# One transformer-block kernel: the rings of split weights begin 64 bytes later than the activations, modulo 128

## What is computed

```
mod = silu(c) @ W_ada + b                      # six vectors of 2048
h   = rmsnorm(x) * (1 + scale1) + shift1
P   = h @ W_in                                 # 2048 x 4944
      -> 8 attention heads (low-rank q and kv, softmax over 512 keys)
      -> 4 mLSTM heads, forward and backward, chunk 128
x   = x + gate1 * (concat(heads) @ W_out)      # 2048 x 2048
h2  = rmsnorm(x) * (1 + scale2) + shift2
x   = x + gate2 * (relu(h2 @ W1)^2 @ W2)       # 2048 x 8192, 8192 x 2048
```

## Time and profile before

| | us |
|---|---|
| median of 2 runs | 2275.3 (2273.9 and 2276.7) |
| span of the profiled execution | 2274.7 |
| TensorE busy (PE) in it | 2224.7 |
| weight loads (PEld) in it | 1859.0 |
| GpSimd busy | 1224.3 |
| VectorE busy | 1508.9 |
| ScalarE busy | 859.9 |

### The profile page before, as it was taken

The page is one execution under the profiler, slowest core; times in us unless marked ns, Lnnn a source line. Parts: engine busy times, 40 slices in busy tenths (PEclk is TensorE's granted clock), DMA queues, the critical chain, the costliest instruction groups (busy, mean ns, idle before and its releaser), DMA issues.

```text
span 2274.7 us, 26399 instructions
## 1 busy us (share of the span) xinstructions
PE 2224.7 (98%) x10292; PEld 1859.0 (82%) x10292; DVE 1508.9 (66%) x1506; ACT 859.9 (38%) x1152; POOL 1224.3 (54%) x521
## 2 busy tenths in 40 slices
PE   6999999999998999999999999999999999999999
PEld 6888888888887878888888888888888888888887
DVE  5876976775646687446687677678666556656756
ACT  5435454533356222333333333333333333333331
POOL 2004344342521455267776766777776667676763
PEclk9999999999999999999999999999999999999999
DMA  9966355454636687444443444343433333333342
GB/s 348 319 219 227 127 184 192 146 201 164 240 130 238 245 286 269 141 127 134 130 126 128 128 128 132 121 149 111 130 111 102 108 96 102 112 94 107 101 170 102
DMA packets 185465, 365.52 MB, mean 161 GB/s; under 512 B 15354, under 2 KB 40444, under 8 KB 183296
## 3 DMA queue, kind: packets, MB, share of 16 engines
q1 hardware_dynamic: 176992, 340.79, 45.5%
q10 hardware_dynamic: 8352, 23.07, 2.7%
HBM read 332.33 MB, written 31.48 MB: 160 GB/s over the span
## 4 chain that ended last, share of the span: by engine, by line
PE 87%; DVE 6%; issue 2%; DMA 2%; ACT 1%; POOL 1%; SPq 1%; DVEq 0%; ACTq 0%; POOLq 0%
PE ps L852 19%; PE ps L853 19%; PE ps L854 19%; PE ps L1345 8%; PE ps L1344 8%; PE ps L1346 8%; DVE acc L1967 1%; DMA araw<-in_w_ada 1%; PE ps L886 1%; PE ps L913 1%; PE ps L1142 1%; DVE acc L2018 1%; DVE rt L2278 1%; DVE qn L2270 0%; SPq L459 0%
## 5 line engine op out<-in xcount | busy, mean ns | idle before, releaser
L396 POOL TENSOR_TENSOR wlo<-wraw,whi 128x1024 fp32r<-128x1024 f32 (+3 forms) x112 | 280.8, 2519 | 465.4 <-ACT whi L391 438.3
L844 POOL TENSOR_TENSOR wlo<-wq,whi 128x1024 fp32r<-128x1024 f32 x150 | 387.0, 2582 | 123.6 <-ACT whi L1859 123.6
L844 POOL TENSOR_TENSOR wlo<-wraw,whi 128x1024 fp32r<-128x1024 f32 x132 | 381.2, 2888 | 33.8 <-ACT whi L1859 33.8
L852 PE MATMUL ps<-h2T,whi 128*128 128x512 f32 x1024 | 398.6, 389 | 0.0
L854 PE MATMUL ps<-h2T,wlo 128*128 128x512 f32 x1024 | 398.4, 389 | 0.0
L853 PE MATMUL ps<-h2T,whi 128*128 128x512 f32 x1024 | 398.3, 389 | 0.0
L2612 DVE TENSOR_TENSOR yacc<-ps,yacc 128x1024 f32<-128x1024 f32 x202 | 246.4, 1220 | 215.9 <-PE ps L1346 213.2
L1344 PE MATMUL ps<-whi,ahi 128*128 128x512 f32 x840 | 326.9, 389 | 0.2 <-DVE yacc L2612 0.2
L1346 PE MATMUL ps<-whi,alo 128*128 128x512 f32 x840 | 326.8, 389 | 0.0
L1345 PE MATMUL ps<-wlo,ahi 128*128 128x512 f32 x840 | 326.8, 389 | 0.0
L1859 ACT ACTIVATE whi<-wq 128x1024 fp32r<-128x1024 f32 x150 | 159.1, 1060 | 354.1 <-PE ps L854 223.3
(11 more groups left out here) (340 smaller groups left out, 3995.4 us busy)
## 6 DMA issues: line engine op xcount, KB each, us to landing
araw<-in_w_ada SPq DMA_DIRECT2D x144, 512.0 KB, 5.8
wraw<-in_w_ff SPq DMA_DIRECT2D x136, 512.0 KB, 3.8
wq<-in_w_ff SPq DMA_DIRECT2D x120, 512.0 KB, 4.2
wraw<-in_w_in SPq DMA_DIRECT2D x72, 512.0 KB, 5.8
arawx<-in_w_ada SPq DMA_DIRECT2D x48, 512.0 KB, 4.7
wraw<-in_w_out SPq DMA_DIRECT2D x32, 512.0 KB, 7.0
xnat<-in_x ACTq DMA_DIRECT2D x4, 1024.0 KB, 8.5
xT_d<-xT ACTq DMA_DIRECT2D x1, 4096.0 KB, 13.3
```

The lines of the kernel that those rows point to most:

```text
L396: pool.tensor_tensor(wlo[:, slot, 0:kb, 0:cols], wraw[:, slot, 0:kb, 0:cols], whi[:, slot, 0:kb, 0:cols].bitcast(F), ALU.subtract).then_in ...
L844: pool.tensor_tensor(wlo[:, slot, :, :], raw, whi[:, slot, :, :].bitcast(F), ALU.subtract).then_inc(lo_ready, 1)
L852: pe.matmul(dst, lhs[0], rhs[0], start=start, stop=False)
```

## The change

Two allocations grow. A filler `pad_w` of 64 bytes stands ahead of `wraw`, and each `under_...` tile grows by 64 bytes:

```
+    at(perm, "pad_w", [P, 16])
     wraw = at(perm, "wraw", [P, RING, KB, 512])
     whi = at(perm, "whi", [P, RING, KB, 512], R)
...
             if kb:
-                at(st, f"under_{tiles[0][0]}", [P, int(kb * 256)])
+                at(st, f"under_{tiles[0][0]}", [P, int(kb * 256) + 16])
             return [at(st, *tile) for tile in tiles]
```

## The result

The changed kernel takes 2318.8 us (median of 2 runs, 2315.6 and 2322.1) against 2275.3: 1.88% slower, ratio 1.0188 with a 95% interval of 1.0171 to 1.0204. It lies 44 us over the forecast and 0.8 us over the top of my range. The profiled execution took 2322.1 us, of which 2320.3 are its span, 45.6 us more than the span of before.

What follows compares the result with a forecast made beforehand. The prediction took TensorE's matmul count times pace as the bound. Its sum, 0 on the matmuls and 0 +/- 3 us on the start, left the 2274.7 us span unchanged: forecast 2275 us, range 2266 to 2318.

Steps and rivals of the forecast that it cites:

- Bound: Whole kernel: TensorE's matmuls fill 98% of the span, so time is the number of matmuls times their pace.
- The pace and its bounds: Ring-tile matmuls: a fixed 13.3 ns beside the columns; 8,781 matmuls, effect bounded from -117 to +117 us.
- The term that the sum put at 0: The change's effect on the pace of the ring-tile matmuls, taken as 0 us.
- Why zero between those bounds: Ring-tile matmuls: two arguments that a start 64 bytes different leaves the pace unchanged, 0 us.
- The first: Load and stream in ring matmuls: their distance drifts some 530 bytes per load, passing every distance modulo 128 about four times.
- The second leg: Transposes from `ckv`, half its rows off by 64: 110 ns each against 109 from aligned `cq`, so no slower load.
- 0.80: Chance given to no change for the whole kernel, at 2268 to 2283 us.
- The rule of two independent ports: TensorE has two independent read ports and never waits on anyone, so the shift is worth 0 us.
- The 96 us: Possible gain on 8,781 matmuls if 10.9 ns each above the formula's 215.8 were contention cured by the shift.
- What else moves: ScalarE, GpSimd, VectorE and clock unaffected; DMA in the start phase 0 with a margin of 3 us.
- The slower one: Shift brings collisions to ring matmuls: persisting 231 ns pace, 40 us, 2315 us, chance 0.06; doubled fixed part 2392 us.
- The faster rival: Fixed part of ring matmuls shrinks: 2158 us if all 13.3 ns go, 2217 if half; chance 0.08.

Runs made afterwards that it cites:

- the probe: Layer left out, series of 64 matmuls alone at varied distances and column counts; with 448 columns 202.5 ns at distance 0, 202.2 at 64.
- e1: Against the kernel before, ring tiles and activation tiles all moved by 64 bytes, distance still 0; 2274.5 us.
- e6: Against the kernel before, rings in place, activation tiles moved by 256 bytes; 2275.7 us.
- e2: Against the kernel before, rings in place, activation tiles moved by 64 bytes; 2316.5 us.
- e3: Against the kernel before, rings in place, activation tiles moved by 128 bytes; 2322.0 us.
- e7: Against the kernel before, only the high ring tile `whi` (with the small tables behind it) moved by 64 bytes; 2320.2 us.
- The bf16 series: Two series of 64 matmuls alone in bf16, layer left out, at distances 0 and 64; 215.9 ns a matmul at 64, starts 215 to 216 apart at 0.

## Why the prediction was wrong

**Bound.** Right. The time is the number of matmuls times their pace, and 39 of the 45.6 us are that pace.

**The pace and its bounds.** Right as far as the rows went: 13.3 ns beside the columns at 336, 384 and 512, none at half clock, and bounds from -117 to +117 us, inside which the +45.6 us lies. As a rule for any number of columns it is not right: the probe has 15.9 ns at 448. The term that the sum put at 0 measured 4.7 ns a matmul, 39 us.

**Why zero between those bounds.** This is the step that failed, in both its legs. The first said that two streams which drift through every distance in one load can't care where they start. The runs show that they do: e1 and e6 against e2, e3 and the change. The argument looks at one matmul and its load by themselves. The runs show that one feeds into the next. At a distance of 0 the starts, once settled, lie 226 or 227 ns apart; at others they fall into cycles of two or three, 231 and 236 ns in turn where the ring is streamed. In e7 the aligned pair between two others is the slowest. The last sentence of my prediction named an exception, a collision at the very start of each load; that the drift argument had a gap was right, but no run shows where in a load the delay arises. The second leg took the transposes from `ckv` as the nearest row. I had noted that a delayed stream would be hidden in them; the probe shows it: with 192 or fewer streamed columns the distances run alike, at 112 ns. So the nearest row could say nothing, and 0.80 stood on one argument.

**The rule of two independent ports.** The Trainium skill, SBUF — State Buffer, section "Who interferes with whom", was read in the prediction as making the shift worth nothing. That reading did not hold: in float32r the pace of the matmuls depends on where the load beside the stream starts. Whether the two read ports themselves disturb each other, or something behind them, no run here shows. The 215.8 ns come from the formula of the Trainium skill, TensorE: Matmul & The Clock Gate, section "Back-to-back issue gap", which that section gives for the gap of an isolated matmul, not for a stream of loads and matmuls as here; the prediction left that condition out. The bf16 series meets it all the same (215.9 ns), float32r at no distance. The 96 us that it seemed to leave open were not found by placement: 226.7 ns is the least of all distances tried at 512 columns.

**What else moves.** Right: GpSimd, VectorE and the DMA shares are as before, no wait of any size was added, and e1 shows the rings' new places free of cost.

**Rivals.** The slower one carried the case. Its price of 4.5 ns, taken from the nine matmuls behind a run of transposes, came to 2315 us, and 2318.8 was measured. That agreement is partly luck: the matmuls don't stay in the 231 ns of those rows but settle at 233.3 or 228.9, and it is the mix of the two that averages 231.6. I gave it 0.06; the right row was in the trace, and it showed that this pace can be 4.5 ns longer for a while with no wait in front of it. The faster rival is excluded for every distance tried, and the rule "distance modulo 128" on which both sides of the prediction stood is wrong: 128 costs as much as 64 (e3), and 256 nothing (e6).

## What to carry to other kernels

Where float32r matmuls of 512 columns run back to back, each with its own weight load of 128, read the start-to-start time at full clock. 226.7 ns is the aligned pace. A lasting 229 to 234 can mean that the tiles loaded and the tiles streamed start at different places modulo 256 bytes, and in this kernel fillers of 64 bytes decide over 1.9% of the time. A short run at 231 just behind other matmuls is no sign of it; the kernel before has that too. Keep all of the tiles on one residue modulo 256, not just most: moving one tile of three cost as much as moving all. With other numbers of columns measure first, for the loss is 3 ns at 384 and none at 448 or 320. And before a row is taken as nearest evidence, ask whether the effect could show in it at all.

## What the runs showed of the hardware that I had not expected

- The pace of float32r matmuls of 512 columns depends on the distance of the two operands' starts modulo 256 bytes: 226.7 ns at 0 and 256, 226.8 at 16 with the loaded one ahead, 229 at 192, 232 to 234 at 32, 64, 96 and 128 (probes). A loaded start 8 bytes off costs 4 ns, a streamed start 16 off 5 ns.
- The loads keep their 188 ns at every distance tried, within 2 ns; bf16 shows no loss at a distance of 64; at half clock the one stretch read, at a distance of 192, shows none (426.7 ns after, 426 before).
- The effect is uneven in the streamed columns (6.7 ns at 512, none at 448, 3 at 384, none at 320), and at 256 columns its sign turns: 117.8 ns at a distance of 64 against 120.0.
- One placement can have two settled paces (228.9 and 233.3 ns for blocks of the same form, behind the same kind of block), in two kernels with the same counts, 56 and 58.

What stays open is the mechanism inside and what selects between two settled paces: nothing here tells a collision in SBUF from one further in, nor what the 13.3 ns of the aligned pace are. That 32 loaded columns don't lower them speaks for a fixed handing-over, but those series ran out of step themselves, at 231.7 ns, so it is not settled. No version beats the kernel before: e1 and e6 equal it within their intervals, and no distance tried in the probes is faster at 512 columns.
